# All six recurrence blocks of a hybrid mixer opened early, and its heads dealt eight and four to two lanes

## The chip, the cores and the metric

One core of one Trainium2 chip runs the whole kernel. The metric is the device time of one execution in microseconds (us), taken as the median of several executions. The engines are TensorE (PE, with its weight loads as PEld), VectorE (DVE), ScalarE (ACT), GpSimd (POOL) and SyncE (SP, which here only issues DMAs).

## The reference

Two parts in float32 on 256 tokens of width 2048, one behind the other: a block of a hybrid mixer, an attention to memory and a convolutional FFN, and then two layers with three kinds of attention side by side. The change touches the hybrid mixer alone:

```python
def hybrid_mixer(h, ...):
    z = h @ w_in
    za, zb, zc = jnp.split(z, [3 * A_WIDTH, 3 * A_WIDTH + 2 * B_WIDTH], axis=-1)
    oa = rmsnorm(dilated_attention(q, k, v), attn_out_gain)      # 12 heads of 64
    ob = rmsnorm(spatial_gating(zb, ...), sgu_out_gain)           # 8 groups of 64
    oc = rwkv7_time_mix(zc, ...)                                  # 12 heads of 64
    return jnp.concatenate([oa, ob, oc], axis=-1) @ w_out

def rwkv7_time_mix(zc, ...):
    zc = zc + (prev - zc) * mu
    r, k, v, w_lo, a_lo, g_lo = jnp.split(zc, cuts, axis=-1)
    decay = jnp.exp(-jnp.exp(-jax.nn.softplus(-(w0 + jnp.tanh(w_lo) @ w_up)) - 0.5))
    a = jax.nn.sigmoid(a0 + a_lo @ a_up)
    kk = k * k_k;  k = k * (1.0 + (a - 1.0) * k_a)
    kk = kk / jnp.maximum(jnp.linalg.norm(kk, axis=-1, keepdims=True), 1e-12)
    y = rwkv7_scan(r, decay, k, v, kk, a)        # state of 64 x 64 per head, step by step
    ...                                          # norm by head, gain, bias, bonus r.k.r_k * v
    return y * (jax.nn.sigmoid(g_lo) @ g_up)
```

## The kernel before

**The products.** `z = h @ w_in` runs as a chain of stages, among them `ST_CE`, `ST_VB`, `ST_B1`, `ST_QK` and `ST_V0`. SyncE loads weights in units of 128 x 2048 numbers. ScalarE rounds a unit to its high half (`w_hi`, line 338), VectorE makes the low half (`w_lo`, line 343), and TensorE multiplies three times (lines 425 to 427). What a stage leaves in PSUM the two engines copy out (their evacuations). `weave(products, fill)` puts one step of another generator, the fill, behind each step of the products. In the kernel before the fill is the token shift of `zc` (`prepare_*`) and the spatial gating (`gating_*`), woven into `ST_B1`, `ST_QK` and `ST_V0`.

**The mixer.** Behind the last product of `ST_V0`, `mixer` runs five lanes with `together`, which gives each generator one step in turn until all are done. A step ends at a `yield`, and one turn over all lanes is called a round here. This is done at build time for each engine apart: the result is a fixed order of instructions on every engine, and each engine works through its own, waiting on semaphores.

- Three recurrence lanes (`recur_*`), with two PSUM banks each, hold blocks 0 to 2 and then 3 to 5. A block is 128 channels, two heads. It first opens: `low` and `lora` (lines 1315, 1317), the sigmoids (1413, 1414), a scan and `kk` on VectorE, the square (1417), `nsum` (1321, 1322), the power -1/2 on GpSimd (856), its spread (1421), `nbc` (1326, 1327), the exponentials (1426 to 1439), `bonus` (1331), and at the end `al`, the last of the opening's products on VectorE. Then come the pair products (1343), copied under a mask (1521), and six levels of a triangular inversion: `xt` (1359), its copy by ScalarE (1449), `m` (1362), its evacuation `U` by VectorE (1534), `n` (1369), and `X` by VectorE (1538). Last come the state and the output (1384 to 1403, with the evacuations 1454, 1460 and 1464).
- Two head lanes, with PSUM banks 2 and 3, hold six of the 12 dilated-attention heads each. A head takes five rounds: scores (1709, 1710), maximum (1748), exponentials (1733), `turned` (1716) and its copy (1738), mixed (1722 to 1724), reciprocal (1754), and `put_aside` (1767). Behind the heads stand finishes of blocks 0 to 2 (`finish_*`: mean 1611 to 1615, variance 1619 and 1621, power on GpSimd, the rest 1624 to 1635), and the attention's norm (`a_norm`: 1105, 1780, 1790, 1793).

The finishes of blocks 3 to 5 (`late_*`) and the opening of `w_out` come behind the mixer. The opening of `w_out` waits for the last step of both head lanes on VectorE.

## Time and profile before

| what | value |
|---|---|
| median of 3 runs | 2358.93 us (2356.34 to 2361.82) |
| the profiled execution | 2356.4 us, its span 2354.7 us, mean granted clock 0.981 |
| TensorE busy | 2267.6 us, 96% of the span |
| VectorE, ScalarE, GpSimd busy | 58%, 45%, 2% |
| last product of `ST_V0` issued to first product of `w_out` | 338.00 to 565.19 us |

Times are microseconds from the span's start. Busy shares are means over all stages. A granted clock of 1.00 is 2.4 GHz, and one near 0.58 means that TensorE ran mostly at 1.2 GHz.

### The profile page before, as it was taken

To read this page: it belongs to the slowest core of one execution; us is meant where nothing else is said; L and a number is where in the kernel's file an instruction comes from. 1 tells how busy PE (TensorE), PEld (TensorE's weight loads), DVE (VectorE), ACT (ScalarE), POOL (GpSimd) and SP (SyncE) were. 2 spreads that over 40 slices of the span, in tenths; PEclk is the share of its full clock that TensorE was granted. 3 is DMA by queue.
4 is the path that set the end of the run, shared out by engine and by line. 5 is a ranking of instruction groups with operands and counts; after the bars stand their busy time and mean duration, and the time that the engine had idled before them with its cause. 6 is when DMAs were issued, how large, how long until landed. Compare 5 with 4: busy or idle time off the path is not lost.

```text
span 2354.7 us, 31774 instructions
## 1 busy us (share of the span) xinstructions
PE 2267.6 (96%) x13038; PEld 1971.1 (84%) x13038; DVE 1359.6 (58%) x1694; ACT 1066.1 (45%) x1375; POOL 58.2 (2%) x66
## 2 busy tenths in 40 slices
PE   8999989899989999999999999999998999999998
PEld 7888978788877888888888888888986889889776
DVE  5444657476566766667676444755445555545554
ACT  4433433323455545454555333545435453544543
POOL 0000020011000000000000000000000000000000
PEclk9999998899999999999999999999999999999999
DMA  7656520013634555555565555554550556445243
GB/s 276 198 173 217 185 89 1 1 32 115 220 114 144 191 183 193 182 194 181 194 199 196 193 189 191 191 191 128 186 179 19 179 179 221 161 149 169 68 128 140
DMA packets 235977, 373.07 MB, mean 158 GB/s; under 512 B 8359, under 2 KB 108244, under 8 KB 235092
## 3 DMA queue, kind: packets, MB, share of 16 engines
q1 hardware_dynamic: 229740, 362.89, 46.9%
q10 hardware_dynamic: 6120, 8.50, 1.0%
q8 instruction: 87, 1.43, 0.3%
q14 instruction: 30, 0.25, 0.0%
HBM read 369.25 MB, written 2.12 MB: 158 GB/s over the span
## 4 chain that ended last, share of the span: by engine, by line
PE 65%; issue 5%; DVE 4%; ACT 2%; POOL 0%; DVEq 0%; POOLq 0%; ACTq 0%
PE PS L466 16%; PE PS L425 12%; PE PS L427 12%; PE PS L426 12%; PE PS L469 8%; DVE w_lo L343 1%; PE PS L1960 1%; ACT w_hi L338 1%; PE PS L2050 1%; PE PS L2034 1%; PE PS L1944 1%; PE PS L905 1%; DVE small L1998 0%; PE PS L2725 0%; ACT spare L1972 0%
## 5 line engine op out<-in xcount | busy, mean ns | idle before, releaser
L343 DVE TENSOR_TENSOR w_lo<-raw,w_hi 128x2048 fp32r<-128x2048 f32 (+2 forms) x340 | 766.4, 2254 | 760.5 <-ACT w_hi L338 760.3
L338 ACT ACTIVATE w_hi<-raw 128x2048 fp32r<-128x2048 f32 (+2 forms) x340 | 641.2, 1886 | 850.9 <-PE PS L427 491.3
L466 PE MATMUL PS<-h_both,w_hi 128*128 128x512 f32 x1968 | 536.5, 394 | 2.9 <-DVE h_both L922 1.8
L425 PE MATMUL PS<-w_hi,h_both 128*128 128x512 f32 (+2 forms) x1344 | 514.8, 383 | 11.3 <-DVE h_both L922 4.6
L426 PE MATMUL PS<-w_lo,h_both 128*128 128x512 f32 (+2 forms) x1344 | 507.2, 377 | 0.0
L427 PE MATMUL PS<-w_hi,h_both 128*128 128x512 f32 (+2 forms) x1088 | 408.0, 375 | 0.0
L466 PEld LDWEIGHTS PS<-h_both,w_hi 128*128 128x128 f32 x1968 | 336.5, 188 | 47.4 <-DVE h_both L922 2.8
L469 PEld LDWEIGHTS PS<-h_both,w_lo 128*128 128x128 f32 x1968 | 301.2, 188 | 42.9
L469 PE MATMUL PS<-h_both,w_lo 128*128 128x256 f32 x1968 | 313.1, 281 | 0.0
L425 PEld LDWEIGHTS PS<-w_hi,h_both 128*128 128x128 f32 x1344 | 254.0, 189 | 59.1 <-DVE h_both L922 5.1
L426 PEld LDWEIGHTS PS<-w_lo,h_both 128*128 128x128 f32 x1344 | 254.2, 189 | 45.5
L427 PEld LDWEIGHTS PS<-w_hi,h_both 128*128 128x128 f32 x1088 | 205.8, 189 | 37.6
L425 PE MATMUL PS<-h_both,w_hi 128*128 128x256 f32 x672 | 194.0, 289 | 4.7 <-DVE w_lo L343 4.6
L426 PE MATMUL PS<-h_both,w_hi 128*128 128x256 f32 x672 | 192.2, 286 | 0.0
L427 PE MATMUL PS<-h_both,w_lo 128*128 128x256 f32 x672 | 192.1, 286 | 0.0
L427 PE MATMUL PS<-w_hi,ff_lo_blocks 128*128 128x512 f32 x352 | 137.0, 389 | 0.0
L425 PEld LDWEIGHTS PS<-h_both,w_hi 128*128 128x128 f32 x672 | 131.1, 195 | 5.7 <-issue 5.3
L426 PEld LDWEIGHTS PS<-h_both,w_hi 128*128 128x128 f32 x672 | 131.2, 195 | 0.0
L427 PEld LDWEIGHTS PS<-h_both,w_lo 128*128 128x128 f32 x672 | 131.1, 195 | 0.0
L427 PEld LDWEIGHTS PS<-w_hi,ff_lo_blocks 128*128 128x128 f32 x352 | 66.1, 188 | 13.7
L856 POOL TENSOR_TENSOR small<-small 128x2 f32<-128x2 f32 (+2 forms) x31 | 29.4, 955 | 1875.5 <-DVE small L828 1048.0
L2177 DVE SCALAR_TENSOR_TENSOR arena<-arena,params 128x255 f32<-128x255 f32 (+1 forms) x176 | 73.2, 479 | 2.8
(523 smaller groups left out, 2045.0 us busy)
## 6 DMA issues: line engine op xcount, KB each, us to landing
raw<-in_w_in SPq DMA_DIRECT2D x132, 1024.0 KB, 5.1
raw<-in_ffn_w_up SPq DMA_DIRECT2D x176, 512.0 KB, 4.3
raw<-in_w_out SPq DMA_DIRECT2D x48, 1024.0 KB, 5.1
raw<-in_ffn_w_down SPq DMA_DIRECT2D x44, 1024.0 KB, 5.0
raw<-in_mem_wkv SPq DMA_DIRECT2D x8, 1024.0 KB, 11.7
raw<-in_mem_wq SPq DMA_DIRECT2D x4, 1024.0 KB, 5.5
raw<-in_mem_wo SPq DMA_DIRECT2D x4, 1024.0 KB, 7.4
raw<-in_w_in SPq DMA_DIRECT2D x4, 768.0 KB, 4.5
```

Source lines behind the costliest of these rows:

```text
L338: act.activation(w_hi[:, slot % 2, :st.n], raw[:, slot, :st.n], ACT.Copy).then_inc(hi_made, 1)
L343: dve.tensor_tensor(w_lo[:, slot % 2, :st.n], raw[:, slot, :st.n], w_hi[:, slot % 2, :st.n].bitcast(F32), ALU.subtract).then_inc(lo_made, 1)
L425: pe.matmul(ps, l_hi, r_hi, start=start, stop=False, skip_group_check=skip)
L426: pe.matmul(ps, l_hi, r_lo, start=False, stop=False, skip_group_check=skip)
L427: return pe.matmul(ps, l_lo, r_hi, start=False, stop=stop, skip_group_check=skip)
L466: pe.matmul(sums, wh[:, k, cs], h_both[:, :, kk, :], start=kk == 0, stop=False, skip_group_check=True)
L469: last = pe.matmul(sums[:, 0, :], wl[:, k, cs], h_hi[:, kk, :], start=False, stop=kk == end, skip_group_check=True)
L856: return pool.tensor_tensor(c, c, minus_half.to_broadcast([P, n]), ALU.pow)
L905: last = pe.transpose(PS[:, turn_bank(n), at:at + P], block(t, k), ident[:, :])
L1944: last = pe.matmul(PS[:, bank, t_ * S:(t_ + 1) * S], q[:, t_ * P:(t_ + 1) * P], k, start=m == 0, stop=m == len(job["pairs"]) - 1)
L1960: last = pe.matmul(PS[:, bank, t_ * P:(t_ + 1) * P], s_[:, (kb * TB + t_) * P:(kb * TB + t_ + 1) * P], job["v"][:, kb, :], start=kb == 0, ...
L2177: last = dve.scalar_tensor_tensor(out=d, in0=rows_up[:, q.parity, m, :S - back], scalar=channel("conv_w", q.g, half, c, 2 - back), in1=d, ...
```

## The change

**Openings.** The opening leaves the recurrence's generators and becomes `open_*`, with rooms and a PSUM bank of its own. Blocks 0 to 2 open in the fill, in banks 6, 7 and 5, staggered by two steps (`EARLY`). The fill now starts at `ST_VB`, so that the shift, the gating and these three openings stand beside the products of four stages. Blocks 3 to 5 open one after another in the second head lane, in bank 3, six rounds each, before that lane's heads. The recurrence lanes go from the sixth level of blocks 0 to 2 and their output straight to the pairs of blocks 3 to 5: 19 rounds a block. On TensorE `lora` now waits for the block's own `low`.

**Heads.** Heads 0 to 7 stand in the first head lane, 8 to 11 in the second. The pauses are gone, and every head puts aside in its own lane. The first lane ends with the finish of block 2 and the norm, the second with the finishes of blocks 0 and 1.

**Loads and GpSimd.** The masks come earlier and into another place, the small matrices for `low` and `lora` are loaded a second time into an early room, and most of GpSimd's clearing moves ahead of the last products.

```diff
+        def open_tensor(pe, j):
+            u0, u1, B = j.room["u0"], j.room["u1"], j.bank
+            if j.first:
+                pe.wait_ge(lora_early, 64)
+                pe.wait_ge(prep.act, prep["tanh"])
+                if j.b == 2:
+                    pe.wait_ge(sgu.act, sgu["w1c"])
+                up, at = z_v[:, 0, :], j.b * P
+            else:
+                pe.wait_ge(lora_in, 48)
+                if j.b == 3:
+                    pe.wait_ge(act_evac, ST_V0.G1)
+                    pe.wait_ge(dve_evac, ST_V0.G1)
+                else:
+                    pe.wait_ge(j.dve, j.dve0)
+                up, at = raw_flat, LORA + j.b * P
+            pe.matmul(PS[:, B, 0:S], up[0:HD, at:at + P], zc[0:HD, 18, :], start=True, stop=True).then_inc(j.pe, 1)
+            pe.wait_ge(j.pe, j["low"])
+            pe.matmul(PS[:, B, S:2 * S], up[HD:P, at:at + P], zc[HD:P, 18, :], start=True, stop=True).then_inc(j.pe, 1)
+            yield
+            pe.wait_ge(j.act, j["sq"])
+            pe.matmul(PS[:, B, 0:2], u0[:, 0:P], j.two, start=True, stop=True)
+            pe.matmul(PS[:, B, 2:4], u0[:, P:2 * P], j.two, start=True, stop=True).then_inc(j.pe, 1)
+            yield
+            pe.wait_ge(j.act, j["nb"])
+            pe.matmul(PS[:, B, 0:P], u1[:, 0:P], ident[:, :], start=True, stop=True)
+            pe.matmul(PS[:, B, P:2 * P], u1[:, P:2 * P], ident[:, :], start=True, stop=True).then_inc(j.pe, 1)
+            yield
+            pe.wait_ge(j.dve, j["ru"])
+            for t_ in range(TB):
+                pe.matmul(PS[:, B, S + 2 * t_:S + 2 * t_ + 2], u0[:, t_ * P:(t_ + 1) * P], j.two, start=True,
+                          stop=True).then_inc(j.pe, 1)
+            yield
+
...
+        def v0_scalar(act, q):
+            act.wait_ge(rk_opens[2].pe, rk_opens[2]["lora"])
+            act.wait_ge(rk_opens[2].dve, rk_opens[2]["l1"])
+            v0_to_scalar(act, q)
+
+        def v0_vector(dve, q):
+            dve.wait_ge(rk_opens[1].dve, rk_opens[1]["al"])
+            v0_to_vector(dve, q)
+        ST_QK.scalar_evac, ST_QK.vector_evac = qk_scalar, qk_vector
+        ST_V0.scalar_evac, ST_V0.vector_evac = v0_scalar, v0_vector
+        EARLY = (0, 2, 4)
+
+        def opened(part, e, pauses):
+            return together(*[after(n, spaced(part(e, rk_opens[b]), pauses)) for b, n in enumerate(EARLY)])
+
+        def opened_tensor(pe):
+            return opened(open_tensor, pe, (1, 2, 2, 1))
+
+        def opened_scalar(act):
+            return opened(open_scalar, act, (3, 0, 2, 2, 0))
+
...
-        HEADS_FIRST, TO_FIRST, TO_SECOND, HEAD_ROUNDS = 8, 3, 5, 5
-        LANE_JOBS = [[Pause(TO_FIRST)] + side_jobs[0:HEADS_FIRST:2] + [Pause(TO_SECOND)] + side_jobs[HEADS_FIRST::2]
-                     + [finishes[0], finishes[2]],
-                     [Pause(TO_FIRST)] + side_jobs[1:HEADS_FIRST:2] + [Pause(TO_SECOND)] + side_jobs[HEADS_FIRST + 1::2]
-                     + [a_norm, finishes[1]]]
-        PUT_FIRST = (0, 1, HEADS_FIRST, HEADS_FIRST + 1)
+        a_norm = Steps(head_lanes[0]["chain"], act="sq", pool="rstd", dve="sq1 mean x0 x1")
+        a_norm.kind, a_norm.lane, a_norm.ssq, a_norm.rstd = "norm", head_lanes[0], col(2), col(2)
+        LANE_JOBS = [side_jobs[:HEADS_FIRST] + [finishes[2], a_norm],
+                     [rk_opens[b] for b in range(3, CB)] + side_jobs[HEADS_FIRST:] + finishes[0:2]]
+        LAST_HEADS = side_jobs[HEADS_FIRST - 1], side_jobs[-1]
...
+        def later_tensor(pe, j):
+            yield from spaced(open_tensor(pe, j), (0, 0, 1, 0))
+            yield
+
+        def later_scalar(act, j):
+            yield from spaced(open_scalar(act, j), (0, 0, 0, 1, 0))
+
+        def later_vector(dve, j):
+            opening = open_vector(dve, j)
+            yield
+            next(opening)
+            yield
+            next(opening)
+            next(opening)
+            yield
+            yield
+            next(opening)
+            yield
+            next(opening)
+            yield
+
+        def later_gpsimd(pool, j):
+            yield
+            yield
+            norm_gpsimd(pool, j)
+            yield from rounds(4)
 
         def side_tensor(pe, j):
-            if j.kind == "pause":
...
+            for st in (ST_C, ST_CE):
                 run(products_tensor(pe, st))
-            fill = prepare_tensor(pe)
-            weave(products_tensor(pe, ST_B1), fill)
-            fill = together(fill, gating_tensor(pe))
-            weave(products_tensor(pe, ST_QK), fill)
-            weave(products_tensor(pe, ST_V0), fill)
+            fill = together(prepare_tensor(pe), after(4, gating_tensor(pe)), after(4, opened_tensor(pe)))
+            for st in (ST_VB, ST_B1, ST_QK, ST_V0):
+                weave(products_tensor(pe, st), fill)
             run(fill)
...
             rows_gpsimd(pool, n_mem)
             rows_gpsimd(pool, n_x)
-            gating_gpsimd(pool)
+            gating = gating_gpsimd(pool)
+            next(gating)
+            norm_gpsimd(pool, rk_opens[0])
+            norm_gpsimd(pool, rk_opens[1])
+            next(gating)
+            norm_gpsimd(pool, rk_opens[2])
+            run(gating)
+            for n, (lane, zero) in enumerate(zip(rk_lanes, zeros)):
+                pool.wait_ge(unit_used, ST_V0.U1 - (2 if n == 0 else 1))
+                pool.memset(lane["mats"], 0.0).then_inc(zero.pool, 1)
+                pool.wait_ge(zero.pool, zero["products"])
+                pool.tensor_scalar(lane["mats"][:, :, 0, :], bc4(ident[:, :]), -1.0, None, ALU.mult).then_inc(zero.pool, 1)
+                if n == 0:
+                    pool.wait_ge(masks_in, 32)
+                    for mask in (level_mask(0), level0_t):
+                        pool.tensor_tensor(mask, mask, ident[:, :], ALU.subtract).then_inc(rk_start.pool, 1)
```

**Where the instructions stand.** Three places, as the built programs have them. `PS` is PSUM, and `arena`, `raw_flat`, `side` and `spare` are the program's regions of SBUF.

TensorE at the first opening, before: the blocks go through `nsum` (lines 1321, 1322) and `nbc` (1326, 1327) with nothing between them, and the first head's scores (1709, 1710) follow. The rows begin with the second block's `nsum`.

```order
L1321 MATMUL PS<-raw_flat 128x2
L1322 MATMUL PS<-raw_flat 128x2
L1321 MATMUL PS<-raw_flat,spare 128x2
L1322 MATMUL PS<-raw_flat,spare 128x2
L1326 MATMUL PS<-ident,side 128x128
L1327 MATMUL PS<-ident,side 128x128
L1326 MATMUL PS<-ident,raw_flat 128x128
L1327 MATMUL PS<-ident,raw_flat 128x128
L1326 MATMUL PS<-ident,spare 128x128
L1327 MATMUL PS<-ident,spare 128x128
L1709 MATMUL PS<-arena 128x128
L1710 MATMUL PS<-arena,exch 128x128
```

TensorE after, at the start of the mixer: `low` and `lora` of block 3 (lines 1346, 1348) stand between the first and the second half of the pairs (1513), its `nsum` (1351, 1352) between the pairs and the transposes that follow (1519 to 1522). Its `nbc` comes behind the first level.

```order
L1346 MATMUL PS<-arena,raw_flat 128x256
L1348 MATMUL PS<-arena,raw_flat 128x256
L1513 MATMUL PS<-arena 128x128 x24
L1351 MATMUL PS<-raw_flat,spare 128x2
L1352 MATMUL PS<-raw_flat,spare 128x2
L1519 MATMUL PS<-ident,arena 128x128
L1520 MATMUL PS<-ident,arena 128x128
L1522 MATMUL PS<-ident,side 128x128 x4
L1519 MATMUL PS<-ident,arena 128x128
```

The openings of blocks 0 to 2 have left this place for the products; one opening at a time now stands between recurrence work.

ScalarE before, in the last level of blocks 3 to 5 and behind it: the copies of `xt` (1449) and the evacuations of the state and output part (1454, 1460, 1454) follow each other, with one square of a finish (1597) ahead.

```order
L1449 ACTIVATE spare<-PS 128x512
L1597 ACTIVATE spare<-raw_flat 128x256
L1449 ACTIVATE side<-PS 128x512
L1449 ACTIVATE raw_flat<-PS 128x512
L1449 ACTIVATE spare<-PS 128x512
L1454 ACTIVATE side<-PS 128x128
L1454 ACTIVATE raw_flat<-PS 128x128
L1454 ACTIVATE spare<-PS 128x128
L1460 ACTIVATE side<-PS,small 64x64 x4
L1460 ACTIVATE arena<-PS,small 64x64 x2
L1454 ACTIVATE side<-PS 128x128
```

ScalarE after, at the same place behind the last level of blocks 0 to 2: the same evacuations have lines 1594, 1600, 1594 now, and between them stand a table load, a head's exponentials (1814) and those of block 5 (1383, 1390, 1394).

```order
L1594 ACTIVATE side<-PS 128x128
L1594 ACTIVATE raw_flat<-PS 128x128
L1594 ACTIVATE spare<-PS 128x128
L1600 ACTIVATE side<-PS,small 64x64 x4
L1600 ACTIVATE arena<-PS,small 64x64 x2
L1814 ACT_TABLE_LOAD
L1814 ACTIVATE spare,small<-PS,small 128x128
L1814 ACTIVATE spare,small<-PS,small 128x256
L1383 ACTIVATE small<-small 128x1
L1390 ACTIVATE spare<-spare,small 128x128 x2
L1394 ACTIVATE spare<-spare,small 128x128 x2
L1594 ACTIVATE side<-PS 128x128
```

The exponentials of an opening and of a head, with a table load, moved in between two evacuations for which TensorE waits.

VectorE before, in round two: a finish (1611 to 1615) and the norm (1105, 1790, 1793) stand between the levels (1534, 1538).

```order
L1611 TENSOR_REDUCE small<-raw_flat 128x4
L1613 TENSOR_SCALAR small<-small 128x4
L1615 TENSOR_TENSOR raw_flat<-raw_flat,small 128x2x128
L1767 TENSOR_SCALAR arena<-PS,small 128x64 x2
L1105 SCALAR_TENSOR_TENSOR arena,small<-arena 128x768
L1790 TENSOR_SCALAR small<-small 128x2
L1793 TENSOR_SCALAR arena<-arena,small 128x768 x2
L1534 TENSOR_TENSOR side<-PS,spare 128x512
L1534 TENSOR_TENSOR raw_flat<-PS,spare 128x512
L1534 TENSOR_TENSOR spare<-PS,spare 128x512
L1611 TENSOR_REDUCE small<-raw_flat 128x4
```

VectorE after: everything of the finishes (lines 1699 to 1723) stands behind the recurrence's last copies (1640).

```order
L1640 COPY spare<-PS 128x128
L1829 TENSOR_REDUCE small<-PS 128x1 x2
L1831 TENSOR_SCALAR small<-small 128x2
L1835 RECIPROCAL small<-small 128x2 x2
L1850 TENSOR_SCALAR arena<-PS,small 128x64 x2
L1699 TENSOR_REDUCE small<-raw_flat 128x4
L1701 TENSOR_SCALAR small<-small 128x4
L1703 TENSOR_TENSOR raw_flat<-raw_flat,small 128x2x128
L1850 TENSOR_SCALAR arena<-PS,small 128x64 x2
L1699 TENSOR_REDUCE small<-raw_flat 128x4
L1701 TENSOR_SCALAR small<-small 128x4
L1703 TENSOR_TENSOR raw_flat<-raw_flat,small 128x2x128
```

The finishes and the norm (1121, 1873, 1876, further on) moved out from among the levels and stand ahead of the late finishes and of the opening of `w_out`.

## Rows read from the trace of the kernel before

**Rows 1.** The page, part 1, TensorE; part 5, the high halves on ScalarE.

```profile
PE 2267.6 (96%) x13038; PEld 1971.1 (84%) x13038; DVE 1359.6 (58%) x1694; ACT 1066.1 (45%) x1375; POOL 58.2 (2%) x66
...
L338 ACT ACTIVATE w_hi<-raw 128x2048 fp32r<-128x2048 f32 (+2 forms) x340 | 641.2, 1886 | 850.9 <-PE PS L427 491.3
```

**Rows 2.** Busy time by stretch: length, each engine busy (instructions), granted clock, DMA.

```profile
338.24:365.72 27.48, 19.20 (x75) 14.60 (x73) 19.20 (x56) 14.79 (x47) 14.39 (x14) 0.59 0.18 58
365.72:431.39 65.67, 65.53 (x559) 59.92 (x559) 44.26 (x96) 17.93 (x50) 0.00 (x0) 0.99 0.00 1
431.39:452.37 20.98, 18.27 (x152) 17.16 (x150) 3.83 (x14) 5.18 (x18) 0.00 (x0) 1.00 0.00 1
452.37:474.48 22.11, 18.69 (x73) 14.36 (x71) 13.76 (x54) 15.37 (x48) 3.06 (x3) 0.58 0.00 1
474.48:538.37 63.89, 60.20 (x534) 57.58 (x533) 50.27 (x109) 15.34 (x37) 7.96 (x10) 0.96 0.10 30
538.37:557.58 19.21, 16.38 (x134) 15.23 (x132) 5.82 (x16) 4.42 (x16) 2.91 (x4) 1.00 0.05 8
557.58:565.19 7.61, 4.78 (x42) 4.46 (x40) 6.07 (x13) 7.39 (x14) 3.72 (x5) 1.00 0.45 141
```

**Rows 3.** Timeline of TensorE, first opening: start, length, line, work, [idle before].

```profile
343.02 0.38 PE L1321 MATMUL PS<-raw_flat,side 128*128 128x2 f32 x2 [1.84 <-ACT side L1417]
...
351.38 0.80 PE L1326 MATMUL PS<-ident,side 128*128 128x128 f32 x2 [3.85 <-ACT side L1421]
```

**Rows 4.** Timeline of TensorE, first round at full clock.

```profile
376.26 0.48 PE L1709 MATMUL PS<-arena 64*128 64x128 f32 x2
...
380.35 1.05 PE L1362 MATMUL PS<-side 128*128 128x128 f32 x8
```

**Rows 5.** Timeline of VectorE, the masked copies of the first pairs.

```profile
367.76 2.59 DVE L1521 COPY_PREDICATED side<-spare,PS 128x512 f32<-128x512 int32 x4
...
374.04 1.36 DVE L1521 COPY_PREDICATED spare<-spare,PS 128x512 f32<-128x512 int32 x2
```

**Rows 6.** Timeline of TensorE, round two, the longest wait.

```profile
510.73 2.07 PE L1369 MATMUL PS<-side 128*128 128x128 f32 x8 [2.49 <-DVE side L1534]
```

**Rows 7.** Timeline of ScalarE, the gating part during the products.

```profile
262.57 1.90 ACT L338 ACTIVATE w_hi<-raw 128x2048 fp32r<-128x2048 f32 x1
264.50 1.28 ACT L1145 ACT_TABLE_LOAD   x1
265.79 2.01 ACT L1145 ACTIVATE arena<-arena 128x1024 f32<-128x1024 f32 x2
```

**Rows 8.** Timeline of ScalarE: exponentials of an opening; of two heads.

```profile
464.05 0.68 ACT L1433 ACTIVATE side<-raw_flat,small 128x128 f32<-128x128 f32 x2
...
380.50 0.37 ACT L1733 ACTIVATE spare<-PS,small 128x128 f32<-128x128 f32 x1 [4.19 <-DVE small L1750]
...
381.41 0.37 ACT L1733 ACTIVATE arena<-PS,small 128x128 f32<-128x128 f32 x1
```

**Rows 9.** Timeline of VectorE, finish parts and the norm between the blocks.

```profile
508.93 1.15 DVE L1793 TENSOR_SCALAR arena<-arena,small 128x768 f32<-128x768 f32 x2 [0.82 <-POOL small L856]
...
511.79 0.41 DVE L1611 TENSOR_REDUCE small<-raw_flat 128x4 f32<-128x256 f32 x1
...
512.84 0.69 DVE L1538 TENSOR_TENSOR side<-side,PS 128x512 f32<-128x512 f32 x1
...
520.79 0.41 DVE L1624 TENSOR_TENSOR raw_flat<-raw_flat,small 128x256 f32<-128x256 f32 x1
...
522.70 0.41 DVE L1619 TENSOR_REDUCE small<-arena 128x4 f32<-128x256 f32 x1
```

**Rows 10.** Timeline of GpSimd, one power of a finish.

```profile
516.60 1.02 POOL L856 TENSOR_TENSOR small<-small 128x4 f32<-128x4 f32 x1 [4.80 <-DVE small L1621]
```

**Rows 11.** Timeline of TensorE, the end of the mixer.

```profile
557.35 0.39 PE L1403 MATMUL PS<-arena 128*128 128x128 f32 x2
...
565.19 0.73 PE L425 MATMUL PS<-w_hi,h_both 128*128 128x512 f32 x1 [2.14 <-DVE h_both L922]
```

More of the change, by code:

```diff
@@ L114, in run, with rounds, after, spaced @@
         pass
+def rounds(n):
+    for _ in range(n):
+        yield
+def after(n, part):
+    yield from rounds(n)
+    yield from part
+def spaced(part, pauses):
+    for n in pauses:
+        yield from rounds(n)
+        next(part, None)
+        yield
 def one_by_one(parts):
@@ L1163, in gating_vector @@
             st = sgu_stats
-            for n in range(2):
-                yield
-                yield
-            yield
+            yield from rounds(6)
             for t_ in range(TB):
@@ L1266, in hybrid_two_blocks @@
         rk_jobs = {}
+        open_chain = Chain(new, "rk_open")
+        OPEN_BANK = 3
+        OPEN = dict(pe="low lora nsum nbc bonus0 bonus", act="sig_e sig_a sq nb end f0 f1 g0 g1 h0 h1 hh", pool="npow",
+                    dve="l0 l1 kk ka kmod nmax kkn ru akk plus minus end0 end1 bon be kE rg al")
+        late_u = (sp_(7168, 2, S), sp_(7680, 2, S), sp_(2816, 2, S))
+        rk_opens = {}
         for b in range(CB):
@@ L1547, in recur_vector, with norm_gpsimd @@
             yield
+        def norm_gpsimd(pool, j):
+            pool.wait_ge(j.dve, j["nmax"])
+            power_minus_half(pool, j.norm, 2 * TB).then_inc(j.pool, 1)
         def recur_gpsimd(pool, j):
-            lane = j.lane
-            yield
-            yield
-            pool.wait_ge(j.dve, j["nmax"])
-            power_minus_half(pool, lane["norm"], 2 * TB).then_inc(j.pool, 1)
-            yield
-            for _ in range(6):
-                yield
-            for l in range(1, 7):
-                yield
-                yield
-            for _ in range(4):
-                yield
+            yield from rounds(22)
         def by_head(ap):
@@ L1764, in put_aside @@
             dve.wait_ge(j.dve, j["recip"])
+            if h in (0, HEADS_FIRST):
+                for b in range(3):
+                    dve.wait_ge(rk_opens[b].dve, rk_opens[b]["al"])
             for t_ in range(TB):
@@ L3036, in lanes_made, with mixer @@
                 e.wait_ge(j.dve, j.dve1)
-        def mixer(e, recur, side, first=iter(())):
-            run(together(first, *[one_by_one([recur(e, rk_jobs[b]) for b in (i, i + 3)]) for i in range(3)],
+        def mixer(e, recur, side):
+            run(together(*[one_by_one([recur(e, rk_jobs[b]) for b in (i, i + 3)]) for i in range(3)],
                          *[one_by_one([side(e, j) for j in jobs]) for jobs in LANE_JOBS]))
@@ L3181, in _ @@
             run(products_scalar(act, ST_CE, before=end_of(ST_C), more=True))
-            run(products_scalar(act, ST_VB, before=end_of(ST_CE), more=True))
             act.wait_ge(rel_back, 16)
@@ L3262, in _ @@
             run(products_vector(dve, ST_CE, before=end_of(ST_C), more=True))
-            run(products_vector(dve, ST_VB, before=end_of(ST_CE), more=True))
-            fill = prepare_vector(dve)
-            weave(products_vector(dve, ST_B1, before=end_of(ST_VB), more=True), fill)
-            fill = together(fill, gating_vector(dve))
-            weave(products_vector(dve, ST_QK, before=end_of(ST_B1), more=True), fill)
-            weave(products_vector(dve, ST_V0, before=end_of(ST_QK)), fill)
-            run(fill)
             dve.tensor_scalar(one_minus_ka, params[:, PARAM_AT["k_a"]:PARAM_AT["k_a"] + CB], -1.0, 1.0, ALU.mult,
                               ALU.add).then_inc(rk_start.dve, 1)
-            mixer(dve, recur_vector, side_vector, put_first_vector(dve))
+            fill = together(prepare_vector(dve), after(4, gating_vector(dve)), after(4, opened_vector(dve)))
+            before = ST_CE
+            for st in (ST_VB, ST_B1, ST_QK, ST_V0):
+                weave(products_vector(dve, st, before=end_of(before), more=True), fill)
+                before = st
+            run(fill)
+            last_vector(dve, end_of(ST_V0))
+            mixer(dve, recur_vector, side_vector)
             run(products_vector(dve, ST_OUT,
```

462 lines of the change are left out of this document (236 added, 226 removed).

## The prediction

> **What bounds the kernel now.** The page comes first: TensorE is busy for 96% of the span, while the rounding of weights leaves ScalarE idle for 850.9 us, more than it works on it [rows 1]. So product stages are bound by TensorE, and other engines can take work there as long as their queues are not late. The windows over the mixer come next [rows 2]. Its seven stretches, A to G from here on, run from the last product of `ST_V0` to the first of `w_out`, and sum to 226.95 us. Two are poor: the openings A and D, 27.48 and 22.11 us, with TensorE busy 19.20 and 18.69 us at a granted clock of 0.59 and 0.58. A busy share does not show this, since an engine at 1.2 GHz is as busy as one at 2.4. The timeline names the waits in them: 1.84 us for the squares, 3.85 us for the spread of the power [rows 3]. B is full (65.53 of 65.67 us). E is nearly full, with some clock lost. The last stretch G, from the last output product to the first of `w_out`, takes 7.61 us.
>
> **Openings 0 to 2 among the products (A).** At full clock A's TensorE work is 19.20 x 0.59 = 11.3 us. The transposes of `vt`, which stay, are 0.45 us (estimated, as four of 128 x 128), and the scores of two heads take 4.09 us [rows 4]; with 0.66 us for the two turned ones, 6.1 us are left for three openings. They don't vanish: products run at full clock and bind, so each instruction put between them costs its own time. The new wait of `lora` for `low` has no row here. From below it is nothing, and from above it is the 1.84 us of [rows 3], a wait that goes through another engine. I take 0.6 us a block, nearer to nothing because no second engine takes part: 8.0 us in all. Switching between products and small matmuls gets 0.7 us. ScalarE's gelu unit now has two table loads of 1.28 us around its 2.01 us [rows 7], behind an evacuation by VectorE, so that its next high half comes about a unit late. I price that at 1.0 us, between nothing and the 5.4 us that a unit takes TensorE (estimated). Then the pairs wait 1.05 us for the evacuation of the last products. A goes from 27.48 to **11.2 us**. GpSimd's clearing (14.39 us busy in A [rows 2]) is off the path.
>
> **Openings 3 to 5 in bank 3 (D, B).** D loses its openings; only the scores of one head are left, 4.09 / 2 = **2.1 us** for 22.11. But `nsum` of block 3 stands behind the pairs on TensorE, and its square waits for `kk`, which stands on VectorE behind twelve masked copies. They start at 367.76 us, 2 us after the pairs, and the last two, of 1.36 us, start at 374.04 us [rows 5]: 7.6 us in a row. With a maximum, a scan and `kk` behind them, the square is ready some 13 us into the round. TensorE has 8.7 us of work for that time: a gap of 4.4 us. Transposes and the first level, which need nothing of block 3, stand behind it. A gap of 2.49 us was followed by matmuls of twice the length [rows 6]: eight took 2.07 us, where the eight at 380.35 us took 1.05 [rows 4]. I add 3.3 us for that. In the levels, `U` waits once for the copies of `xt` that stand on ScalarE behind an opening's exponentials (0.68 us for each pair of halves, 1.28 together) and a head's (0.91 us [rows 8]): 2.65 us, with 1.6 us of clock behind it and 0.65 us of small waits. B's own matmuls lose one head's scores and gain parts of openings: 62.3 us. B becomes 62.3 + 4.4 + 3.3 + 2.65 + 1.6 + 0.65 = **74.9 us** (65.67 before).
>
> **The output of blocks 0 to 2 (C).** Before, C is 20.98 us with 18.27 us of TensorE. Now a head's turned and mixed products and parts of block 5's opening come in, 22.4 us in all. On ScalarE a table load of 1.28 us [rows 7], a head's exponentials of 0.91 us and an opening's of 1.28 us [rows 8] stand between the evacuations: 3.5 us, nearly all on the path since each output step waits for the one before. With 1.0 us of clock: **26.9 us**.
>
> Here a page speaks against the change. The row shows a load of 1.28 us, begun 0.03 us after the previous operation ends, the next operation 0.01 us behind it, and no drain [rows 7]. The Trainium skill, page "ScalarE: Activation LUTs", section "What ACT_TABLE_LOAD costs", gives 1283 ns for the load and about 1380 ns of drain for every switch to another set, 2.66 us together. By its figure this part would be about 1.4 us longer. By the row it is as above.
>
> **Round two (E, F).** The finishes and the norm leave it. The gap of 2.49 us [rows 6] was VectorE's: two puts of the norm (1.15 us) and a finish [rows 9] stood ahead of `U`. E's matmuls are 60.2 us [rows 2], some 2.2 of it lost to the clock (0.96 of 63.89 us), so 58.0. Two more heads are left for this part, at 4.09 / 2 = 2.05 us for scores [rows 4] and 1.0 for turned and mixed, estimated from their matmuls of 128 x 128: 58.0 + 6.1, with 0.2 us of waits, is **64.3 us** (63.89 before). F gets two more scores and one head's turned and mixed products: 19.21 + 4.1 + 1.1 = **24.4 us**.
>
> **The tail (G).** Lane one needs 40 rounds for its heads, and lane two 18 for openings and 20 for heads, while the recurrence is done in 38. So all three finishes and the norm come behind the last output product, on VectorE in this order, and the late finishes and the opening of `w_out` behind them. VectorE's own time, from [rows 9]: four puts of two, 1.6 us until the first finish; three starts at 1.05 us (511.79 to 512.84); three variances at 0.55; three rests at 1.91 (520.79 to 522.70); the norm, 1.15 and 1.13 for its square and mean. That is 1.6 + 3.15 + 1.65 + 5.73 + 2.28 = 14.4 us. GpSimd's powers of 1.02 us [rows 10], with hand-over both ways, and ScalarE's squares are exposed four times for about 1.25 us: 19.4 us. Two late starts, which had lain beside the recurrence's output, add 2.1 us, and 0.9 us of the old G disappears. G goes from 7.61 [rows 11] to **28.2 us**. Nothing on TensorE covers it: it has only mixed products, transposes and gates there, some 5 us.
>
> **The sum.** 11.2 + 74.9 + 26.9 + 2.1 + 64.3 + 24.4 + 28.2 = 232.0 us against 226.95: +5.1 us. What 36 us of openings give is handed back in the tail (20.6), B (9.2), C (5.9), F (5.2) and E (0.4). The profiled execution took 2356.4 us, 2.5 below the median; 2361.5 in its terms is **2364** in the median's. I count less than 0.2% (4.7 us) as no difference that a measurement of this kernel can tell.
>
> **Rivals.**
> (1) *The waits inside the rounds don't bind* (the other side). I read them from positions in queues, not from rows. The traces of before show B without a wait at all [rows 2], with the same masked copies. If `nsum`, the last `U` and C's evacuations find their operands ready, 4.4 + 3.3 + 2.65 + 1.6 + 3.5 = 15.5 us go, and with some of it left the time is about 2351. It decides from 5 us: less of them than that, and the kernel is faster by more than 5.
> (2) *The products stall.* The fill stands on ScalarE and VectorE behind and ahead of rounding, over four stages. If six units come late by 1.3 us (one table load [rows 7]) in place of the 1.0 us in all, +7: 2372. The idle time in [rows 1] speaks against it, the fixed order for it.
> (3) *The tail is covered*, so that the finishes run beside the last levels' gaps as before: 15 to 20 us less, 2346. The order of VectorE speaks against it; only if the recurrence's end were late itself would it be so.
> (4) *Table switches cost more than the load.* Ten loads stand from the gating to the end of the mixer where five stood. If three of the new ones on the path cost 1.4 us each beyond their row, +4: 2368. This is the time that the Trainium skill's page named above would give; the trace disagrees with it.
>
> **How the numbers follow.** My forecast has 50%, (1) 24%, (2) 15%, (3) 5%, (4) 6%. Slower by over 0.2% is over 2363.6: about half of my own case (27%), (2) and (4), 48%. Faster is under 2354.2: 18% of (1), (3), and 3% of mine, 26%. The rest, 26%, is within. The range 2349 to 2375 leaves out (3) and the far ends of (1) and (2), about 18%; the forecast's own is 2357 to 2371.
>
> **What would show it.** In the trace of after: nearly no wait of TensorE in the four product stages, and 11 us from the last product to the first pair; a gap of 4 us ahead of line 1351 with the clock down behind it; one of 2 to 3 us at line 1539 in the last level; waits ahead of the output products for 1594; no clock near 0.58 for 20 us anywhere; and 28 us without products at the end, with the chain on VectorE's lines 1699 to 1723 and GpSimd's power. I am wrong if B has no gap over 2 us, or if the tail is under 20 us (faster), or if the product stages before 338 us are longer by over 12 us (slower).

## The result, and the profile after

The changed kernel takes 2373.32 us (median of 4, 2372.69 to 2374.88) where the kernel before took 2358.89 us (4 runs, 2356.34 to 2361.82): 1.0062 times as long, interval 1.0049 to 1.0074, or 14.4 us more. The forecast was 2364.0 with a range of 2349 to 2375.

The windows of the changed kernel, cut at the same instructions as [rows 2] and with the same columns. The first row runs from the end of its last `ST_V0` product to the first pair.

```profile
347.89:348.88 0.99, 0.16 (x2) 0.04 (x1) 0.69 (x1) 0.78 (x2) 0.91 (x2) 1.00 0.00 0
348.88:424.02 75.14, 68.26 (x553) 63.08 (x554) 48.18 (x110) 28.83 (x66) 4.12 (x7) 0.93 0.00 1
424.02:451.64 27.62, 21.15 (x153) 19.03 (x151) 7.13 (x26) 8.40 (x29) 0.00 (x0) 0.94 0.11 39
451.64:453.82 2.18, 2.18 (x10) 1.18 (x8) 0.00 (x0) 0.83 (x3) 0.00 (x0) 1.00 0.00 0
453.82:526.18 72.36, 68.76 (x566) 62.92 (x566) 42.05 (x88) 17.87 (x48) 0.00 (x0) 0.95 0.00 1
526.18:548.25 22.07, 19.36 (x151) 17.48 (x150) 4.95 (x18) 6.38 (x25) 0.00 (x0) 1.00 0.05 7
548.25:578.32 30.07, 12.36 (x82) 11.41 (x80) 22.95 (x55) 9.70 (x19) 16.35 (x18) 0.72 0.11 35
```

Its products end 9.65 us later than before (at 347.89 us, not 338.24). With that as part of A, the stretches stand against the forecast like this:

| stretch | before | forecast | measured |
|---|---|---|---|
| A, products' growth and wait for the pairs | 27.48 | 11.2 | 10.64 |
| B, pairs and levels of blocks 0 to 2 | 65.67 | 74.9 | 75.14 |
| C, their output | 20.98 | 26.9 | 27.62 |
| D, up to the pairs of blocks 3 to 5 | 22.11 | 2.1 | 2.18 |
| E, their pairs and levels | 63.89 | 64.3 | 72.36 |
| F, their output | 19.21 | 24.4 | 22.07 |
| G, tail up to `w_out` | 7.61 | 28.2 | 30.07 |

The measured ones sum to 240.1 us, 13.1 more than before and 8.1 more than forecast, and E alone is 8.1 over its forecast. (The profiled spans differ by 16.4 us. The other 3.3 lie behind the first product of `w_out`, where nothing is changed; the fifth run below shows them to be the spread of one execution.)

TensorE's waits in the timeline of the changed kernel, columns as in [rows 3]. These are seven of its longest.

```profile
361.65 0.58 PE L1351 MATMUL PS<-raw_flat,spare 128*128 128x2 f32 x2 [3.90 <-ACT spare L1375]
...
409.23 1.92 PE L1539 MATMUL PS<-side 128*128 128x128 f32 x8 [2.33 <-DVE side L1631]
...
438.74 0.71 PE L1559 MATMUL PS<-side 128*128 128x128 f32 x4 [3.36 <-ACT side L1594]
...
463.60 0.49 PE L1790 MATMUL PS<-arena 64*128 64x128 f32 x2 [3.08 <-DVE arena L1850]
...
557.61 2.04 PE L1673 MATMUL PS<-raw_flat,arena 128*128 128x128 f32 x8 [3.95 <-DVE arena L1723]
...
569.97 3.54 PE L922 MATMUL PS<-ident,arena 128*128 128x128 f32 x16 [10.32 <-DVE arena L1723]
...
578.32 0.51 PE L442 MATMUL PS<-w_hi,h_both 128*128 128x512 f32 x1 [2.13 <-DVE h_both L939]
```

The reader is to see four kinds. At 361.65 and 463.60 us TensorE stands at the start of a round of pairs, and the windows give B and E a granted clock of 0.93 and 0.95. At 409.23 us, in the last level, it waits for the evacuation `U` (1631). That stands on VectorE behind a product of block 4's opening (1448), which had itself waited 3.70 us for the opening's last exponential on ScalarE (1400). At 438.74 us ScalarE's evacuation 1594 is late. From 557.61 us on TensorE waits for VectorE's finishes, 14 us in two waits alone.

The start of the first round on VectorE and ScalarE, same columns: the last six of the twelve masked copies (line 1618) stand as one block of 3.8 us, from 355.79 us on, and `kk` (1415) and the square (1375) come behind them. (The first six start at 350.14 us.)

```profile
355.79 2.56 DVE L1618 COPY_PREDICATED side<-raw_flat,PS 128x512 f32<-128x512 int32 x4 [1.88 <-PE PS L1513]
...
358.24 1.32 DVE L1618 COPY_PREDICATED spare<-raw_flat,PS 128x512 f32<-128x512 int32 x2
...
360.81 0.33 DVE L1415 TENSOR_SCALAR side<-arena,params 128x256 f32<-128x256 f32 x1
...
360.30 0.37 ACT L1814 ACTIVATE spare<-PS,small 128x128 f32<-128x128 f32 x1 [3.05 <-DVE small L1831]
...
361.18 0.42 ACT L1375 ACTIVATE spare<-side 128x256 f32<-128x256 f32 x1
```

The square starts as `kk` ends (361.14 us); the head's exponentials ahead of it on ScalarE end at about the same time. The square ends at 361.60 us, and `nsum` starts at 361.65. It was the chain that the prediction named, with a gap of 3.90 us where it said 4.4.

### The profile page after: what moved, and what is told of

It reads as the page before. It is cut to its first block, busy times and chain, and to the rows that moved or that the text cites. A ratio compares the mean times of both kernels' runs of the same rounds, so it can differ in the third digit from the quotient of the medians.

```text
span 2371.1 us, 31811 instructions
## 1 busy us (share of the span) xinstructions
PE 2268.8 (96%) x13038; PEld 1971.6 (83%) x13038; DVE 1360.7 (57%) x1694; ACT 1072.0 (45%) x1380; POOL 63.1 (3%) x66
## 4 chain that ended last, share of the span: by engine, by line
PE 85%; DVE 6%; issue 5%; ACT 2%; POOL 0%; DMA 0%; ACTq 0%; DVEq 0%; SPq 0%; POOLq 0%
PE PS L483 19%; PE PS L442 15%; PE PS L444 15%; PE PS L443 15%; PE PS L486 10%; DVE w_lo L360 1%; PE PS L1539 1%; PE PS L1532 1%; ACT w_hi L355 1%; PE PS L2056 1%; PE PS L922 1%; PE PS L2146 1%; PE PS L2130 1%; PE PS L1529 1%; PE PS L2040 1%
```

## The experiments

All numbers in the fences have the columns of [rows 2] or [rows 3]. The line numbers are those of each kernel itself. Where small differences count, the stretches of the traces are compared, since whole executions of the kernel before spread from 2350.6 to 2362.1 us in this study.

**First run: `nsum` a round later on TensorE.**

```diff
-            yield from spaced(open_tensor(pe, j), (0, 0, 1, 0))
+            yield from spaced(open_tensor(pe, j), (0, 1, 0, 0))
```

> On TensorE alone, nsum of blocks 3 to 5 stands one round later. Theory (nsum's own chain holds the queue): the wait of 3.90 us at line 1351 shrinks to what the masked copies leave, about 1 us, and the clock behind it drops less, so 3 to 6 us off 2373.3: about 2369. Rival (the masked copies of VectorE are the bound there, and nsum only stands in front): the same wait moves to the transposes at line 1519, the sum stays within 1.5 us. A second rival: the levels wait for nmax behind nsum, and it gets slower by 1 to 3 us.

Measured: 2374.12 us (5 runs, 2368.78 to 2376.82) beside 2356.57 of before, ratio 1.0068 (1.0055 to 1.0082). No gain against the change. The first theory had the wait right and not the time; neither had the reason. The timeline of TensorE and the windows of B and of 27 us of the output part, this kernel's and then the changed one's:

```profile
361.80 0.55 PE L1797 MATMUL PS<-ident,spare 128*128 128x128 f32 x3 [0.78 <-ACT spare L1814]
...
367.76 0.49 PE L1355 MATMUL PS<-ident,spare 128*128 128x128 f32 x2 [1.27 <-ACT spare L1379]
...
421.95 0.71 PE L1559 MATMUL PS<-side 128*128 128x128 f32 x4 [1.40 <-ACT side L1594]
...
439.17 1.22 PE L1559 MATMUL PS<-side 128*128 128x128 f32 x4 [3.07 <-ACT side L1594]
...
349.39:419.86 70.47, 64.50 (x554) 58.22 (x554) 46.86 (x108) 27.99 (x65) 3.12 (x6) 1.00 0.01 1
425.00:452.00 27.00, 22.07 (x124) 19.52 (x124) 5.93 (x23) 7.86 (x27) 0.00 (x0) 0.70 0.13 40
...
425.00:452.00 27.00, 20.90 (x149) 18.87 (x149) 7.13 (x26) 8.28 (x29) 0.00 (x0) 0.94 0.12 40
```

The wait of 3.90 us is gone, nothing of it moved to the transposes, and B is 70.47 us, not 75.14: 4.7 us shorter, with its clock at 1.00. But a wait of 1.40 us now stands ahead of the output part, and there the granted clock falls to 0.70 where the change had 0.94. The output part gives back all that B won: C takes 33.2 us in place of 27.62. So a wait costs its own length and the clock behind it, and here the second part showed up again behind the next waits. That it moved there is read from one trace of each kernel. The third and the sixth run below have the same instructions and the same waits in C, at granted clocks of 0.94 and 1.00, so a part of such a difference can be chance. That nothing was won in the sum is shown by all five executions.

**Second run: finishes 0 and 1 ahead of heads 8 to 11** (and the norm three rounds later, so that it stands behind head 11).

```diff
-                     [rk_opens[b] for b in range(3, CB)] + side_jobs[HEADS_FIRST:] + finishes[0:2]]
+                     [rk_opens[b] for b in range(3, CB)] + finishes[0:2] + side_jobs[HEADS_FIRST:]]
...
```

> The finishes of blocks 0 and 1 stand ahead of heads 8 to 11 in the second head lane, and the norm three rounds later. Theory (the tail is long because the side lanes have more rounds than the recurrence, whatever stands last): the tail from the last output product to w_out stays 26 to 32 us, now with the chain of the last two heads in it, and the time is within 4 us of 2373.3. Rival (the tail is the finishes' work on VectorE): with two of three finishes out of it, it is 8 to 10 us shorter, about 2364.

Measured: 2372.31 us (5 runs, 2370.41 to 2373.54), ratio to before 1.0064 (1.0050 to 1.0077), 1.0 us under the changed kernel. The tail, and the waits in it:

```profile
549.29:575.59 26.30, 14.93 (x86) 12.44 (x84) 17.13 (x44) 11.56 (x27) 11.70 (x12) 0.74 0.12 40
...
538.96 0.49 PE L1798 MATMUL PS<-arena 64*128 64x128 f32 x2 [1.50 <-DVE arena L1858]
...
559.17 0.90 PE L1805 MATMUL PS<-ident,spare 128*128 128x128 f32 x3 [1.87 <-ACT spare L1822]
...
567.11 3.65 PE L922 MATMUL PS<-ident,arena 128*128 128x128 f32 x16 [4.82 <-DVE arena L1887]
```

It is 26.30 us where the change has 30.07. Two of three finishes are out of it, and heads' chains (line 1805 waits for the exponentials) stand there instead. The tail stays in the 26 to 32 us of the theory: lanes of 40 and 38 rounds leave nothing of the 38 rounds of recurrence for what comes behind them, and what stands last matters for 4 us. Even these are not won, since F, the output ahead of the tail, is 27.71 us here (521.58 to 549.29) and 22.07 in the change.

**Third run: the early openings alone.** Blocks 3 to 5 open in their own lanes and banks between their two blocks; heads six and six, finishes and norm as before.

```diff
-            o = Steps(open_chain if inside else lane["chain"], **OPEN)
+            o = Steps(lane["chain"], **OPEN)
...
-            o.bank = (6, 7, 5)[b] if o.first else OPEN_BANK
+            o.bank = (6, 7, 5)[b] if o.first else lane["banks"][1]
...
-            run(together(*[one_by_one([recur(e, rk_jobs[b]) for b in (i, i + 3)]) for i in range(3)],
+            run(together(*[one_by_one([recur(e, rk_jobs[i]), later(e, rk_opens[i + 3]), recur(e, rk_jobs[i + 3])])
+                           for i in range(3)],
...
+        HEADS_FIRST, TO_FIRST, TO_SECOND = 8, 0, 5
+        LANE_JOBS = [[Pause(TO_FIRST)] + side_jobs[0:HEADS_FIRST:2] + [Pause(TO_SECOND)] + side_jobs[HEADS_FIRST::2]
+                     + [finishes[0], finishes[2]],
+                     [Pause(TO_FIRST)] + side_jobs[1:HEADS_FIRST:2] + [Pause(TO_SECOND)] + side_jobs[HEADS_FIRST + 1::2]
+                     + [a_norm, finishes[1]]]
```

> One part alone: blocks 0 to 2 open beside the products as in the change, but blocks 3 to 5 open in their own recurrence lanes and banks as before, heads are dealt six and six, and the finishes and the norm stand in round two again. Theory (the early openings pay by themselves, and the rest gives back more than it takes): 9.7 us more of products, 16 us less of mixer opening with the second opening, the rounds and the tail as before (22, 64 and 8 us): about 16 us under the kernel before, 2343, range 2338 to 2350. Rival (the openings beside the products hurt more than they show): not under 2354.

Measured: 2353.15 us (11 runs, 2350.92 to 2356.76) beside 2356.57, ratio 0.9981 (0.9972 to 0.9990). Faster than before, though by 3.4 us and not by 16: it lies outside the range of the theory and within 1 us of the rival's bound. Its windows B to G:

```profile
347.92:415.54 67.62, 66.12 (x565) 59.57 (x565) 41.17 (x84) 17.32 (x48) 1.06 (x4) 1.00 0.01 1
415.54:443.39 27.85, 22.65 (x156) 19.68 (x154) 5.42 (x20) 6.01 (x24) 0.00 (x0) 0.94 0.00 1
443.39:461.52 18.13, 11.97 (x62) 9.73 (x61) 12.41 (x50) 13.70 (x40) 3.08 (x3) 0.73 0.08 13
461.52:529.81 68.29, 64.83 (x554) 59.78 (x555) 49.95 (x109) 17.25 (x46) 6.93 (x9) 0.97 0.04 13
529.81:549.38 19.57, 16.35 (x134) 15.23 (x132) 8.31 (x23) 4.71 (x17) 3.92 (x5) 1.00 0.04 7
549.38:556.63 7.25, 4.78 (x42) 4.46 (x41) 6.08 (x13) 7.03 (x13) 5.69 (x5) 1.00 0.44 142
```

The tail is 7.25 us, as expected, and the second opening 18.13, 4.0 us less than before, where 22 was expected. B, C and E are 67.62, 27.85 and 68.29 us, not 65.67, 20.98 and 63.89, together 13.2 us more. In the kernel before, four heads' scores stood in the two openings. Here they are work in C and E: TensorE is busy for 22.65 and 64.83 us there, not 18.27 and 60.20 [rows 2], 9.0 us more, and four scores are 4 x 2.05 = 8.2 us. Most of the rest is waits, the longest 2.08 us in C. `w_out` starts 8.6 us earlier than before, so the early openings of blocks 0 to 2 pay. What loses is the rest of the change, the openings in the second head lane together with the new dealing of heads and finishes: with it the kernel takes 19 to 20 us more than without. No run parts these two.

**Fourth run: half the masked copies left out.** The copies of the second half of the pairs write 8 of 512 columns, so the recurrence's results are not the reference's.

```diff
+                wide = 4 * P if i < 2 else 8
-                dve.copy_predicated(mats[:, i, :, :].rearrange("p m t -> p (m t)"), pair_mask, PS[:, (A, B)[i % 2], :])\
+                dve.copy_predicated(mats[:, i, :, :].rearrange("p m t -> p (m t)")[:, 0:wide], pair_mask[:, 0:wide],
+                                    PS[:, (A, B)[i % 2], 0:wide])\
```

> Left out: the masked copies of the second half of the pairs write 8 columns of 512, so half of VectorE's masked copying is gone and the results of the recurrence are not the reference's. Theory (the 7.7 us of masked copies bound the start of both rounds): the wait at line 1351 falls from 3.90 us to under 1, the wait of 3.08 us for the put in round two goes to nothing, and the half clock behind both goes with them: 10 to 14 us off 2373.3, about 2361. Rival (nsum waits for its own chain over ScalarE's table load, and the put for its head): under 5 us off.

Measured: 2366.31 us (5 runs, 2364.34 to 2366.74), 7.0 us under the changed kernel, between the theory's 10 to 14 and the rival's 5.

```profile
359.29 0.38 PE L1351 MATMUL PS<-raw_flat,spare 128*128 128x2 f32 x2 [2.32 <-ACT spare L1375]
...
456.60 0.49 PE L1791 MATMUL PS<-arena 64*128 64x128 f32 x2 [0.71 <-DVE arena L1851]
```

The wait in round two falls from 3.08 to 0.71 us, so there the copies are the cause: E is 67.62 us with its granted clock at 1.00, where the change has 72.36 and 0.95. The wait for `nsum` falls only from 3.90 to 2.32, and B from 75.14 to 71.30 us. Behind the copies it has a chain of its own, the maxima, a scan and `kk` on VectorE and then the square on ScalarE, which starts at 358.82 us as `kk` ends. Both theories hold a part.

**Fifth run: the kernel before, once more.**

> The kernel before, profiled once more. From the first product of w_out to the end its first trace shows 1789.5 us, that of the change 1792.8, though no instruction there is changed. If that is the spread of one execution, this trace shows a value between them or above; if the change makes the rest slower, it shows 1789 to 1790 again.

Measured: 2361.69 us, span 2360.0. Its first product of `w_out` starts at 565.57 us (565.19 in the first trace), so the mixer repeats within 0.4 us, and the part behind it takes 1794.43 us, not 1789.51. The change's 1792.78 lies between. So the 3.3 us behind the mixer are spread, and the change costs what the stretches show, 13.1 us.

**Sixth run: `lora` of blocks 3 to 5 in the lane's other bank**, so that TensorE needs no wait for `low` there; otherwise the third run. (The sigmoid on ScalarE reads the other bank too.)

```diff
-            pe.wait_ge(j.pe, j["low"])
-            pe.matmul(PS[:, B, S:2 * S], up[HD:P, at:at + P], zc[HD:P, 18, :], ...
+            if j.first:
+                pe.wait_ge(j.pe, j["low"])
+            pe.matmul(PS[:, j.lora_bank, S:2 * S], up[HD:P, at:at + P], zc[HD:P, 18, :], ...
```

> The early openings alone (as the third run), but lora of blocks 3 to 5 goes to the lane's other bank, so that TensorE need not wait for low. Theory (low and lora on two halves of the rows run beside each other only when nothing stands between them): the six matmuls of that opening take 1.5 us instead of 3.0, and the kernel is 1 to 2 us under the third run's 2353.2. Rival (the sigmoids behind them bind): no change within 0.5 us.

Measured: 2354.11 us (11 runs) where the third run had 2353.15, ratio to before 0.9976 (0.9967 to 0.9985). The six matmuls do shrink, from 3.0 us (from 443.48 us on) to 1.5, but the wait for the square behind them grows from 0.64 to 2.18 us. The rival holds.

**Seventh run: the sixth, with the second four heads two rounds earlier.**

```diff
-        HEADS_FIRST, TO_FIRST, TO_SECOND = 8, 0, 5
+        HEADS_FIRST, TO_FIRST, TO_SECOND = 8, 0, 3
```

> The same, and the second four heads begin two rounds earlier (pause of 3 rounds, not 5), so that two scores stand in the waits of the second opening. Theory (the opening's waits at half clock were cover for heads, and what lies in them is free): the second opening stays about 18 us long while the rounds behind lose two scores, 2 to 4 us faster than the run before it, about 2348. Rival (the matmuls at half clock lengthen the opening by what they save later): no change.

Measured: 2354.42 us (11 runs), ratio 0.9985 (0.9974 to 0.9996), no change against the sixth. From the last level of round one to the second pairs it takes 53.2 us instead of 46.8, from there to the last level 63.8 instead of 67.4, and from the last product to `w_out` it is 210.7 us instead of 209.2. The theory falls: scores at half clock lengthen the opening by 6.4 us and save 3.6 later. So the second opening had not been free cover for them in the kernel before either.

**Eighth run: the kernel before, with `lora` waiting for `low`.**

```diff
+            pe.wait_ge(j.pe, j["low"])
             pe.matmul(PS[:, B, S:2 * S], raw_flat[HD:P, LORA + j.b * P:LORA + (j.b + 1) * P], zc[HD:P, 18, :], start=True,
```

> The kernel before with one thing added: lora waits for the block's own low on TensorE, six times. Theory: three openings' six matmuls take 4.4 us instead of 1.5, of which the sigmoids and the table load hide a part; slower by 1 to 4 us. Rival (the wait is nearly free, 0.2 us each): no change that can be told, and rows 0.5 us apart.

Measured: 2358.63 us (11 runs) beside 2360.86, ratio 0.9995 (0.9986 to 1.0004): no change that can be told, as the rival had it, but not for its reason. The two openings of this kernel:

```profile
338.75:362.26 23.51, 16.38 (x75) 12.03 (x74) 17.69 (x54) 14.21 (x44) 14.37 (x14) 0.77 0.20 68
449.54:467.87 18.33, 15.45 (x72) 11.36 (x70) 13.01 (x52) 14.59 (x45) 3.06 (x3) 0.81 0.00 1
```

They are 23.51 and 18.33 us where [rows 2] has 27.48 and 22.11. The six matmuls take 3.5 and 3.1 us there, where the theory had 4.4 and the kernel before has 1.6 (from 339.62 us on). And yet the openings are 4 us shorter each, with a granted clock of 0.77 and 0.81 in place of 0.59 and 0.58; the second trace of the kernel before has 0.60 and 0.59 over the same stretches. From the last product to `w_out` it is 220.5 us instead of 226.95, 6.5 us less. The medians show a third of that; I can't say why, as this is one trace.

**Ninth and tenth run: the sixth, with all heads one round later, and two.**

```diff
-        HEADS_FIRST, TO_FIRST, TO_SECOND = 8, 0, 5
+        HEADS_FIRST, TO_FIRST, TO_SECOND = 8, 1, 4
```

(2 and 3 in the tenth.)

> The kernel of the sixth run with all heads one round later (pauses of 1 and 4 rounds instead of 0 and 5). Two heads' exponentials no longer stand on ScalarE between the evacuations behind the last level. Theory: the wait of 2.08 us for the second evacuation there goes to about 0.37, the span is 1 to 3 us under the sixth run's 2350.1. Rival (the same exponentials stand ahead of another wait then): no change, and a wait of 1.5 to 2.5 us at another line.

> The same with two rounds (pauses of 2 and 3). Theory: the wait of 2.08 us goes as well, but no heads' scores stand beside the masked copies of the first round, so a wait of 2 to 4 us opens ahead of the transposes and the clock may fall behind it: 0 to 4 us over the run with one round. Rival: the masked copies are hidden by the pairs alone, and it equals that run.

Measured: 2347.58 us (5 runs, 2347.18 to 2349.74) beside 2360.38, ratio 0.9954 (0.9941 to 0.9967); and 2351.76 us (6 runs), ratio 0.9964 (0.9952 to 0.9976). The ninth is the fastest of the study. Both are to be compared with the sixth run. On ScalarE of the third run, which stands here like the sixth, and of the changed kernel:

```profile
428.23 0.37 ACT L1818 ACTIVATE spare<-PS,small 128x128 f32<-128x128 f32 x1
...
429.83 0.29 ACT L1592 ACTIVATE side<-PS 128x128 f32<-128x128 f32 x1
...
435.07 1.28 ACT L1814 ACT_TABLE_LOAD   x1
...
436.36 0.37 ACT L1814 ACTIVATE spare<-PS,small 128x128 f32<-128x128 f32 x1
...
438.43 0.26 ACT L1594 ACTIVATE side<-PS 128x128 f32<-128x128 f32 x1
```

In the third run heads' exponentials stand ahead of evacuation 1592 on ScalarE, which starts 1.6 us behind the first of them shown here, and TensorE waits 2.08 us for it, in the third run and in the sixth. In the ninth they don't: that wait is 0.37 us, as expected, and no wait of B is over 0.53 us.

```profile
348.26:414.21 65.95, 64.89 (x553) 58.53 (x553) 41.13 (x84) 17.78 (x48) 1.31 (x4) 1.00 0.01 1
414.21:440.70 26.49, 23.78 (x180) 20.70 (x178) 5.61 (x20) 7.79 (x28) 0.00 (x0) 1.00 0.00 1
440.70:456.65 15.95, 8.46 (x52) 7.72 (x49) 12.66 (x50) 11.85 (x37) 3.09 (x3) 0.76 0.08 17
456.65:525.80 69.15, 65.69 (x554) 60.55 (x555) 49.97 (x109) 17.27 (x46) 6.94 (x9) 0.96 0.03 13
```

The second and third of these rows are cut behind `low` and `lora` of blocks 3 to 5. Cut behind the last output product, as in the tables above, the ninth's C is 24.49 us where the sixth has 26.47, both at a granted clock of 1.00, and its opening 17.95 where the sixth has 18.13. B is 65.95 us, not 67.61; of this, 1.3 us are two heads' mixed products that no longer stand at its end. From the first pairs to the second the ninth takes 108.4 us and the sixth 112.2, more than the 1 to 3 us of the theory. The exponentials were the cause of the wait.

The tenth has no head beside its first masked copies, and yet TensorE waits there only twice, 0.34 us each time, and B is 65.4 us. So the pairs alone hide the copies nearly whole, and the wait of 2 to 4 us that was expected is not there. But from the first pairs to the second the tenth takes 114.1 us. Its waits ahead of the second pairs are like the ninth's (3.36 and 2.88 us, 3.06 and 2.47 there). Its granted clock is not: 0.88 over the 28.43 us of C, where the ninth has 1.00, and 0.70 over the 20.27 us of the opening, where the ninth has 0.79. At full clock the matmuls of the two C would be alike (28.43 x 0.12 = 3.4 us of 24.95 are clock, which leaves 21.5; 21.78 in the ninth). One round later is the better of the two; why the clock falls in the tenth stays open.

## Why the prediction was right, and where it was off

- **Direction.** Slower, as the likeliest case said, for its reason: the tail (30.07 us, forecast 28.2), B (75.14, forecast 74.9) and C (27.62, forecast 26.9) give back more than the openings give. The size was not right: 14.4 us more where the sum added 5.1, and 2.3 us above the 2371 that the forecast gave its own case; only the wider range holds it. Rival 1, that the waits don't bind, failed: they are 3.90, 2.33 and 3.36 us where 4.4, 2.65 and 3.5 were priced. Rival 2 has the nearest time, 2372, but that is luck, since the products did not stall (below under A). Rival 3, a covered tail, failed with 30.07 us.
- **B by its parts.** TensorE's matmuls are 63.0 us at full clock (68.26 busy, less 75.14 x 0.07), waits 6.9, and clock 5.3; priced were 62.3, 7.7 and 4.9. Two things in it were not as told. The wait of 2.33 us was put down to the copies of `xt` (1589 in this kernel) behind exponentials on ScalarE. The last of them starts at 406.04 us, ahead of the exponentials; what is late is VectorE's product 1448, which waits for those exponentials and stands ahead of `U`. And B was said to lose one head's scores, where it lost three (six heads' before, three in the change), while E went from two heads' to six and not to four. The sums of the matmuls came out within 1.2 us all the same, which the prediction does not itemise and which is in part luck.
- **The term that was mis-sized: E.** The step was "58.0 + 6.1, with 0.2 us of waits, is 64.3 us". It measured 72.36. The prediction charged the twelve masked copies to B and not to E, where they start at 455.02 us (3.9 us) and 459.44 us (3.8 us), with a head's put at 463.08 us behind them. TensorE waits 3.08 us for the put, 3.6 us of waits in all, and the clock was 0.72 for 12.4 us behind it (12.4 x 0.28 = 3.5 us). The matmuls were 65.3 us at full clock, 1.2 over. The fourth run shows the copies as the cause of that wait: with half of them left out, 4.7 of the 8.1 us go.
- **A.** The growth of the products was 9.65 us against 8.0 + 0.7 + 1.0, and 0.45 for the transposes of `vt`, which stand among the products too. How it is made up was half right. The new wait of `lora`, taken as 0.6 us a block, costs about 1.0. The timeline of TensorE in `ST_VB` of the changed kernel shows what one `low` and `lora` cost among products:

```profile
234.02 0.39 PE L444 MATMUL PS<-w_hi,h_both 128*128 128x512 f32 x1
...
234.34 0.70 PE L1346 MATMUL PS<-arena 64*128 64x256 f32 x2
...
235.10 0.70 PE L1348 MATMUL PS<-arena 64*128 64x256 f32 x2
...
235.72 0.50 PE L442 MATMUL PS<-w_hi,h_both 128*128 128x512 f32 x1
```

A product was due at 234.25 us, and comes at 235.72: 1.47 us for one block's two, where three blocks' six take 1.5 us beside each other in the sixth run. In the change both write one bank and `lora` waits for `low`, and that overlap is lost. ScalarE's gelu unit, priced at 1.0 us, cost nearly nothing: TensorE waited 0.48 us in the whole 147.89 us from 200 us on, and 0.14 us in the kernel before from 200 us to its last product.
- **The page on the activation tables.** By the Trainium skill ("ScalarE: Activation LUTs", "What ACT_TABLE_LOAD costs") a switch costs 2.66 us with its drain. Here the load at 435.07 us takes 1.28 us and the next operation starts at 436.36; load, one head's exponentials and the opening's fill the time to 438.43 us without a gap. The trace disagrees with the page on the drain, and rival 4 falls.
- **F.** The forecast is 2.3 us too long: of the two heads' scores counted for it, one stood in E.
- **G.** 1.9 us over. Two finishes lost 0.8 and 1.0 us on VectorE beside GpSimd's operations (last section), which the prediction did not price.
- **The clock.** I priced it wait by wait. The first run speaks against that: a wait of 3.90 us taken away left the sum as it was, and the clock fell 60 us later instead.

## What to carry to other kernels

Work moved beside a stage that TensorE bounds costs its full time there, so count what it cost where it was. Four heads' scores that had stood in the openings came back as 9.0 us of work in C and E (third run). But try it before you call a poor stage free cover: two scores put back into the second opening won nothing (seventh run). When side lanes run beside a loop of fixed length, add up their rounds first; what does not fit is a serial tail, whatever is put last. And look for the same block of a slow engine's work in every round of the loop, not only in the first.

## What the runs showed of the hardware

- The granted clock of an opening depends on more than its busy share. With one wait more between `low` and `lora` it was 0.77 and 0.81 (eighth run, one trace), without it 0.59 and 0.58 (0.60 and 0.59 in the fifth run). The opening with the added wait was the shorter by 4 us, and TensorE stood idle for 7.1 us in the first, not 8.3.
- Two traces of the same instructions with the same waits can differ in the granted clock: C had 0.94 over 27.85 us in the third run and 1.00 over 26.47 us in the sixth.
- VectorE's operations of 128 x 256 took up to twice their time where they started behind one of GpSimd's. Two operations of line 1712 in the tail of the changed kernel, the first without GpSimd at work and the second with it:

```profile
555.46 0.42 DVE L1712 TENSOR_TENSOR raw_flat<-raw_flat,small 128x256 f32<-128x256 f32 x1 [1.13 <-POOL small L873]
...
559.12 0.83 DVE L1712 TENSOR_TENSOR raw_flat<-raw_flat,small 128x256 f32<-128x256 f32 x1
...
559.05 0.61 POOL L1734 TENSOR_TENSOR spare<-arena,small 128x256 f32<-128x256 f32 x1
```

The same line takes 0.42 us there and 0.83 us beside GpSimd's operation of the same size. GpSimd's ends at 559.66 us, VectorE's at 559.95, 0.29 us behind it. Where VectorE's starts first nothing is lost: line 1703 at 570.51 us takes 0.42 us, with GpSimd's from 570.60 us on. Two of the finishes lost some 0.8 and 1.0 us in such places; no run tried it apart.
